# Hybrid decoder trunk on one core: factors spread by split products, mixer sums kept as rows, recurrence tiles five apart

## The chip, the core and the metric

The kernel runs on one NeuronCore of a Trainium2 chip. TensorE (PE in the profile) multiplies, VectorE (DVE), ScalarE (ACT) and GpSimd (POOL) do the elementwise work, SyncE (SP) and ACT issue the DMAs. Each engine runs its own queue in order, and the engines wait for each other through semaphores. The metric is the device time of one execution in microseconds (us); less is better.

## The reference

Two layers, each of three sub-layers with an RMSNorm before and after: a SwiGLU feed-forward, a mixer, a second feed-forward. All arithmetic is float32; x has 1024 features, the hidden layer of a feed-forward 2816.

```python
def layer(x, st_h, st_conv, st_gla, reset_first, p):
    h = rmsnorm(x, p['norm_pre'][0])
    x = x + 0.5 * rmsnorm(swiglu(h, gate0, up0, down0), p['norm_post'][0])
    h = rmsnorm(x, p['norm_pre'][1])
    m, h_last, new_conv, S_fin = mixer(h, st_h, st_conv, st_gla, reset_first, p)
    x = x + rmsnorm(m, p['norm_post'][1])
    h = rmsnorm(x, p['norm_pre'][2])
    x = x + 0.5 * rmsnorm(swiglu(h, gate1, up1, down1), p['norm_post'][2])
```

The mixer projects h to 20 blocks of 128 columns and a low-rank part of 16 columns. Blocks 0 to 3 go through a causal convolution of width 4, two block-diagonal gates and a linear recurrence, and are multiplied with GeLU of blocks 4 to 7 and normalized over 512 features. Blocks 8 to 19 are q, k, v and the output gate of a gated linear attention with 4 heads in chunks; its decay comes from the low-rank part; each head's output is normalized over 128 features. Both parts together go through the output projection. There are 512 prompt tokens and 8 sequences of 8 sample tokens.

## The kernel before

**Tokens and operands.** The 576 tokens are split into two groups g of 288. Everything is held transposed: 128 features on the partitions, 288 tokens along the free axis. A float32 product is made of three fp32r products: each operand is split into a rounded part and the rest (`hh` and `hl` for x, `hidh` and `hidl` for the hidden layer, `wh` and `wl` for weights). ACT makes the rounded part of a weight block (`hi`, L694), DVE the rest (`lo`, L957).

**Units and stages.** A unit is one block of 128 output features: 24 fp32r products of 288 columns (21 where the contraction has 7 tiles). Weight blocks come through a ring of 6; `hi` works 4 units ahead and `lo` 3. Three PSUM banks hold unit results, so unit u waits until the result of unit u-3 is taken, by DVE mostly. `stage_order` lays the units out in stages: for each layer three feed-forward pieces of group 0 (`ffn`), then `ffn` of group 1 with the input projection `win` of group 0 (20 units) among them, `wout` of group 0 (8 units), `win` of group 1, `ffn`, and so on.

**Side work.** What is not a unit product is written as generators that take one step (a slot) after each unit, on each engine's own queue: `recurrence` starts with a `win` stage, `attention` behind it, `boundary` after a sub-layer's last stage. A slot's number fixes the place in each queue; nothing is scheduled at run time. In `recurrence` tile t's convolution, gates and scan lie at slots 4t, 4t+3 and 4t+7. In `attention` the chunk's decay factors are made by ACT at `T_FACTORS`, the keys `kf` by DVE at `T_KEYS` and the slot behind, the queries `qf` by POOL at `T_QUERIES`, and PE transposes values and keys at `T_TRANSPOSES`. `take` on DVE reads a unit's result; `act` is SiLU of the gate on ACT, `hid` the product on DVE.

**Norm factors.** ACT squares, POOL adds the squares up in `ssum`. PE turns them into one column of sums per 96 tokens (`columns`, L428), ACT copies them (`cols`), POOL takes the power -1/2 (`inv`), DVE multiplies it into a diagonal matrix (`diagonal`, L970), and PE multiplies ones by that diagonal in plain fp32 (`spread`, L449), which gives the factor of each token on all partitions. The program holds 44 such spreads: 24 for x and y, and five in each of four mixers.

Of the kernel before, what the change touches and what calls it, by code (L numbers as in the profile page):

```python
# [12 lines left out]
P = 128  # L13
D = 1024
# [47 lines left out]
T_QUERIES = (5, 13, 18)  # L62
T_TRANSPOSES = (7, 15, 23)
T_SCORES = (9, 17, 25)
T_OUTPUTS = (12, 20, 27)
T_SUMS = 30
T_VALUES = T_SUMS + 4

# [90 lines left out]
def program(nc, a, ctx):  # L159
# [36 lines left out]
    diag = [sb(f"diag{s}", [TC, NTC, TC]) for s in range(2)]  # L196
    cols = sb("cols", [TC, 5 * NTC])
    inv = sb("inv", [TC, 5 * NTC])
# [8 lines left out]
    ones = sb("ones", [P, P])  # L207
    means = sb("means", [P, 3])
# [12 lines left out]
    wgdh = sb("wgdh", [P, L, DT * RANK], F32R)  # L221
    wgdl = sb("wgdl", [P, L, DT * RANK], F32R)
    wg2 = sb("wg2", [RANK, L, PR * P])
# [26 lines left out]
    squares, val, eb, qe, gd = [], [], [], [], []  # L250
    for g in range(G):
# [3 lines left out]
        gd.append(sb(f"gd{g}", [RANK, T]))  # L255
# [4 lines left out]
        qe.append(sb(f"qe{g}", [P, PR, C]))  # L260
        assert cursor[0] <= result_at[g] + DT * T * 4
        cursor[0] = result_at[g]
        val.append([sb(f"val{g}{s}", [P, T]) for s in (0, 1)])
# [19 lines left out]
    setup_v, setup_a, setup_p, wgdh_ready, wgdl_ready = (sem(k) for k in ("setup_v", "setup_a", "setup_p", "wgdh_ready", "wgdl_ready"))  # L283
    sq_ready, sq_used = [sem(f"sq_ready{g}") for g in range(G)], [sem(f"sq_used{g}") for g in range(G)]
# [22 lines left out]
    y_stored = sem("y_stored")  # L307

# [11 lines left out]
    def shares_adds(l, st, g):  # L320
        return (l, st) == (L - 1, 2) or (st, g) == (0, 1)

# [12 lines left out]
    def pace(s):  # L335
        if s.kind == "ffn" and s.f == 0 and s.g == 1:
            return 0, 8, 2
        if s.kind == "wout" and s.g == 0:
            return 4, 18, 1
        return 1, 15, 1  # L340

# [19 lines left out]
    def _(e):  # L361
        e.dma_start(raw[0][:, 0:depth(0) * P], a[SOURCES[0][0]][SOURCES[0][1], :, :]).then_inc(raw_landed[0], 16)
        e.dma_start(par[:, :], a["par"]).then_inc(par_landed, 16)
        for u in range(1, RING):
            e.dma_start(raw[u][:, 0:depth(u) * P], a[SOURCES[u][0]][SOURCES[u][1], :, :]).then_inc(raw_landed[u], 16)
        for t, src in ((ident, "ident"), (maskf, "masks"), (seqmask, "seqmask"), (cont, "cont"), (sth, "st_h"), (stc, "st_conv"),
# [28 lines left out]
        for g in range(G):  # L395
            for k in range(4):
# [7 lines left out]
    def _(e):  # L404
        sides = Sides()
        last_use = []
        kept = [0]
        group_event = [0, 0]
# [17 lines left out]
        def columns(src, k, at, first, start, stop):  # L426
            for t in range(NTC):
                mm = e.matmul(psS[0:TC, 0, 288 + at + t:289 + at + t], src[:, t * TC:(t + 1) * TC], means[:, k:k + 1],  # L428
# [7 lines left out]
        def token_sums(g, normed=None):  # L436
            sums_free()
            e.wait_ge(sq_used[g], (DT - 1) * (group_event[g] + 1))
            columns(ssum[g], 0, 0, True, True, True).then_inc(cols_ready, 1)
# [7 lines left out]
        def spread(out, k, count):  # L447
            e.wait_ge(diag_ready, count)
            e.matmul(out, ones[0:TC, :], diag[k][:, :, :], start=True, stop=True).then_inc(spread_done, 1)  # L449

        diags = [0]

        def spread_one():
            spread(psS[:, 0, 0:T], diags[0] % 2, diags[0] + 1)
            diags[0] += 1

        def first_norm(g):
# [6 lines left out]
            spread_one()  # L464

        def boundary(l, st, g, timing, final):
            start, end, at_once = timing
            for slot in range(end + 3):
                if slot == start:
                    token_sums(g, 2 * (3 * l + st) + 2)  # L470
                if slot == start + 2:
# [1194 lines left out]
```

## Time and profile before

| | us |
|---|---|
| median of three runs | 2302.16 |
| lowest and highest | 2298.94, 2306.12 |
| profiled execution, its own time | 2302.01 |
| its span, first to last instruction | 2300.2 |
| PE busy (16988 products) | 2252.3 |
| DVE busy | 1371.8 |
| ACT busy | 1172.6 |
| POOL busy | 722.1 |
| mean granted TensorE clock | 0.981 of full speed |

The span is what the profile can explain; 1.8 us lie around it. A product of 288 columns is busy for about 0.3 us, but a new one starts every 0.13 us, so what a group of products costs is read from the chain of work (its length by its count) and not from the busy time of one. A plain fp32 product appears as two records. An entry in brackets behind a row says how long its engine idled before and for whom.

### The profile page before, as it was taken

Reading aid. Unit: us, or ns where it says so; the run is one execution under the profiler, and the core shown is the slowest. Engines: PE = TensorE matmul, PEld = TensorE weight load, DVE = VectorE, ACT = ScalarE, POOL = GpSimd, SP = SyncE. Lnnn points to the kernel's source line nnn. Section 1 sums busy time; section 2 is a strip of 40 time slices with the busy share of each in tenths; the row PEclk is TensorE's granted clock in tenths of the full one; section 3 lists DMA queues with packets and bytes.
Section 4 is the critical chain, followed back from the end, with each engine's and each line's share of the span. In section 5 each row is a group of like instructions: output and inputs, shape, how many; then the busy total and the mean of one; then the engine's idle time right before and its main releaser. Section 6 shows DMA issues by size and latency. Waiting matters only on the chain.

```text
span 2300.2 us, 40598 instructions
## 1 busy us (share of the span) xinstructions
PE 2252.3 (98%) x16988; PEld 2218.3 (96%) x16988; DVE 1371.8 (60%) x1789; ACT 1172.6 (51%) x1820; POOL 722.1 (31%) x746
## 2 busy tenths in 40 slices
PE   8999999999999999999999999999999999999997
PEld 8999999999899999999999999999998999999997
DVE  6555747647786456655574556675577755576454
ACT  6534547435675345543454355574366653454433
POOL 4112503415354224421251124142254522242112
PEclk9999999989999999999999999999899999999998
DMA  6555555335444455555555555543354443555553
GB/s 214 160 164 163 164 165 156 119 111 166 137 147 128 119 169 157 164 164 164 162 162 163 167 162 159 165 154 122 104 172 138 138 129 114 182 156 165 163 166 118
DMA packets 102244, 350.58 MB, mean 152 GB/s; under 512 B 11296, under 2 KB 16416, under 8 KB 102064
## 3 DMA queue, kind: packets, MB, share of 16 engines
q1 hardware_dynamic: 100976, 346.82, 49.4%
q8 instruction: 135, 2.21, 0.4%
q10 hardware_dynamic: 1088, 1.18, 0.1%
q14 instruction: 45, 0.37, 0.0%
HBM read 343.09 MB, written 4.87 MB: 151 GB/s over the span
## 4 chain that ended last, share of the span: by engine, by line
PE 90%; DVE 7%; ACT 1%; issue 1%; DMA 0%; POOL 0%; DVEq 0%; ACTq 0%; POOLq 0%
PE psD L422 84%; DVE wl L957 2%; DVE kf L1125 1%; PE psS L428 1%; DVE hl L993 1%; PE psM L532 1%; PE psS L449 1%; PE psM L592 1%; PE psM L488 1%; PE psM L508 1%; DMA x<-in_xT 0%; PE psM L581 0%; PE psM L610 0%; DVE y L982 0%; PE psM L449 0%
## 5 line engine op out<-in xcount | busy, mean ns | idle before, releaser
L422 PE MATMUL psD<-hh,wh 128*128 128x288 f32 x3712 | 1124.4, 303 | 14.9 <-DVE hl L993 8.2
L422 PE MATMUL psD<-hl,wh 128*128 128x288 f32 x3712 | 1105.1, 298 | 0.0
L422 PE MATMUL psD<-hh,wl 128*128 128x288 f32 x3712 | 1101.3, 297 | 0.0
L957 DVE TENSOR_TENSOR wl<-raw,wh 128x1024 fp32r<-128x1024 f32 (+1 forms) x656 | 824.2, 1257 | 137.1 <-ACT wh L694 136.8
L694 ACT ACTIVATE wh<-raw 128x1024 fp32r<-128x1024 f32 (+1 forms) x656 | 672.8, 1028 | 145.2 <-DMA raw<-in_w_in 61.8
L422 PEld LDWEIGHTS psD<-hh,wh 128*128 128x128 f32 x3712 | 706.2, 190 | 25.8 <-DVE hl L993 11.1
L422 PEld LDWEIGHTS psD<-hl,wh 128*128 128x128 f32 x3712 | 707.0, 190 | 2.5
L422 PEld LDWEIGHTS psD<-hh,wl 128*128 128x128 f32 x3712 | 708.7, 191 | 0.0
L1565 POOL TENSOR_TENSOR hidl<-hid,hidh 128x288 fp32r<-128x288 f32 x176 | 215.6, 1225 | 974.5 <-ACT hidh L914 974.5
L422 PE MATMUL psD<-hidh,wh 128*128 128x288 f32 x1408 | 421.7, 300 | 0.0
L422 PE MATMUL psD<-hidl,wh 128*128 128x288 f32 x1408 | 416.7, 296 | 0.0
L422 PE MATMUL psD<-hidh,wl 128*128 128x288 f32 x1408 | 416.0, 295 | 0.0
L422 PEld LDWEIGHTS psD<-hidh,wh 128*128 128x128 f32 x1408 | 265.3, 188 | 3.6 <-issue 0.7
L422 PEld LDWEIGHTS psD<-hidl,wh 128*128 128x128 f32 x1408 | 265.7, 189 | 0.5
L422 PEld LDWEIGHTS psD<-hidh,wl 128*128 128x128 f32 x1408 | 266.2, 189 | 0.0
L1354 POOL TENSOR_TENSOR ssum<-ssum,sq 128x288 f32<-128x288 f32 x168 | 188.4, 1123 | 188.5 <-ACT sq L706 185.0
L910 ACT ACTIVATE act<-gate 128x288 f32<-128x288 f32 x176 | 78.4, 445 | 326.7 <-DVE gate L963 326.6
L914 ACT ACTIVATE hidh<-hid 128x288 fp32r<-128x288 f32 x176 | 78.3, 445 | 308.3 <-DVE hid L963 308.3
L963 DVE TENSOR_TENSOR hid<-psD,act 128x288 f32<-128x288 f32 x176 | 80.3, 456 | 255.2 <-PE psD L422 255.2
L963 DVE TENSOR_TENSOR gate<-psD,rstd 128x288 f32<-128x288 f32 x176 | 80.4, 457 | 247.6 <-PE psD L422 247.1
L1302 DVE TENSOR_TENSOR y<-psD,y 128x288 f32<-128x288 f32 x128 | 58.6, 457 | 155.6 <-PE psD L422 155.6
L993 DVE SCALAR_TENSOR_TENSOR hl<-x,par,hh 128x288 fp32r<-128x288 f32 x96 | 88.6, 932 | 2.8 <-ACT hh L724 2.8
(177 smaller groups left out, 1455.2 us busy)
## 6 DMA issues: line engine op xcount, KB each, us to landing
raw<-in_w_gu SPq DMA_DIRECT2D x352, 512.0 KB, 3.6
raw<-in_w_d SPq DMA_DIRECT2D x128, 448.0 KB, 3.2
raw<-in_w_in SPq DMA_DIRECT2D x80, 512.0 KB, 3.6
raw<-in_w_d SPq DMA_DIRECT2D x64, 512.0 KB, 3.6
raw<-in_w_out SPq DMA_DIRECT2D x32, 512.0 KB, 3.6
out_yT<-x SPq DMA_DIRECT2D x8, 288.0 KB, 3.2
gates<-in_w_ax SPq DMA_DIRECT2D x4, 512.0 KB, 4.8
S<-in_st_gla SPq DMA_DIRECT2D x4, 512.0 KB, 4.5
```

What stands on the lines that cost most here:

```text
L422: mm = e.matmul(out, w[:, kt * P:(kt + 1) * P], t[:, kt, :], start=(kt == 0 and part == 0), stop=(kt == KT - 1 and part == 2))
L428: mm = e.matmul(psS[0:TC, 0, 288 + at + t:289 + at + t], src[:, t * TC:(t + 1) * TC], means[:, k:k + 1], start=(first and t == 0), stop=st ...
L449: e.matmul(out, ones[0:TC, :], diag[k][:, :, :], start=True, stop=True).then_inc(spread_done, 1)
L694: e.activation(wh[u % RING][:, 0:width], raw[u % RING][:, 0:width], ACT.Copy).then_inc(hi_ready, 1)
L910: e.activation(act[:, :], gate[:, :], ACT.Silu).then_inc(silu_ready, 1)
L914: e.activation(hidh[:, j, :], hid[:, :], ACT.Copy).then_inc(hidh_ready, 1)
L957: e.tensor_tensor(wl[u % RING][:, 0:width], raw[u % RING][:, 0:width], wh[u % RING][:, 0:width].bitcast(F32), ALU.subtract).then_inc(lo_re ...
L963: e.tensor_tensor(out, bank(u), by, ALU.mult).then_inc(out_taken, 1)
L993: e.scalar_tensor_tensor(hl[g][:, m, :], x[g][:, m, :], col(par, l * NPAR + PRE + st * DT + m), hh[g][:, m, :].bitcast(F32), ALU.mult, ALU ...
L1302: e.tensor_tensor(y[g][:, m, :], bank(u), y[g][:, m, :], ALU.add).then_inc(out_taken, 1)
L1354: e.tensor_tensor(ssum[g][:, :], ssum[g][:, :], sq[g][m % 2][:, :], ALU.add).then_inc(sq_used[g], 1)
L1565: e.tensor_tensor(hidl[:, j, :], hid[:, :], hidh[:, j, :].bitcast(F32), ALU.subtract).then_inc(hidl_ready, 1)
```

## The change

Seven edits are made together.

- **Spreads.** POOL splits `inv` into a rounded part and the rest, DVE makes a diagonal twice as wide (`diag` 96x576), and PE multiplies ones by its halves in two fp32r products. In seven places (`is_quick`, and the first norm of group 0) no diagonal is made: PE multiplies `inv`, read with a broadcast operand, by the identity in three plain fp32 products of 96 columns, one slot after the sums instead of two.
- **Mixer sums.** Instead of 24 one-column products PE makes 8 plain fp32 products of 288 columns whose weights are 5 columns wide, which put five rows of sums into PSUM; ACT copies them, and three transposes one slot later make columns of them.
- **Low rank.** The rounded part and the rest of the 16 weight columns stand side by side, so that 16 products do what 24 did.
- **Recurrence.** Tiles are five units apart instead of four (`R_PERIOD`), with the blocks of `win` in another order. The last tile's work now reaches past the 20 slots of `win`.
- **Attention.** Queries, transposes, scores, outputs and sums come one slot later; values are made two in a slot.
- **Start.** The first two pieces of x are issued by SP behind the first weight block, the parameters and the last two pieces by ACT; 12 warm-up products go.
- **End.** The last square goes straight to PE instead of through POOL's sum, y is rescaled in four pieces, ACT issues the last two stores, and 22 products keep PE going.

```diff
-WARM_UP = [512] * 16 + [256] * 12
+WARM_UP = [512] * 16
+TAIL_WARM = [256] * 12, [256] * 10
-W_IN_ORDER = [0, 4, 8, 9, 1, 5, 10, 11, 2, 6, 7, 16, 3, 17, 18, 19, 12, 13, 14, 15]
+W_IN_ORDER = [0, 8, 9, 10, 11, 1, 4, 5, 6, 7, 2, 16, 17, 18, 19, 3, 12, 13, 14, 15]
+R_PERIOD = 5
+R_END = R_PERIOD * (LT - 1) + 7
-T_QUERIES = (5, 13, 18)
-T_TRANSPOSES = (7, 15, 23)
+T_QUERIES = (6, 14, 18)
+T_TRANSPOSES = (8, 16, 24)
...
+    def is_quick(l, st, g):
+        return (st, g) == (0, 1) or is_final(l, st)
...
         if s.kind == "wout" and s.g == 0:
-            return 4, 18, 1
+            return 3, 18, 1
...
+        def spread(out):
+            k = diags[0] % 2
+            diags[0] += 1
+            e.wait_ge(diag_ready, diags[0])
+            e.matmul(out, ones[0:TC, :], diag[k][:, 0, :, :], start=True, stop=False)
+            e.matmul(out, ones[0:TC, :], diag[k][:, 1, :, :], start=False, stop=True).then_inc(spread_done, 1)
+
+        def spread_quick():
+            e.wait_ge(inv_ready, event[0])
+            for t in range(NTC):
+                mm = e.matmul(psS[:, 0, t * TC:(t + 1) * TC], inv[:, t:t + 1].broadcast_to([TC, P]), ident[0:TC, 0:TC],
+                              start=(t == 0), stop=True, skip_group_check=True)
+            mm.then_inc(spread_done, 1)
...
             for kt in range(DT):
-                for part, (w, t) in enumerate([(wgdh, hh[g]), (wgdh, hl[g]), (wgdl, hh[g])]):
-                    mm = e.matmul(psM[0:RANK, 3, 0:T], w[:, l, kt * RANK:(kt + 1) * RANK], t[:, kt, :],
-                                  start=(kt == 0 and part == 0), stop=(kt == DT - 1 and part == 2))
+                e.matmul(psM[0:2 * RANK, 3, 0:T], wgp[:, l, kt, :], hh[g][:, kt, :], start=(kt == 0), stop=(kt == DT - 1),
+                         skip_group_check=True)
+                mm = e.matmul(psM[0:RANK, 3, 0:T], wgp[:, l, kt, 0:RANK], hl[g][:, kt, :], start=False, stop=(kt == DT - 1),
+                              skip_group_check=True)
...
                     for t in range(LT):
-                        columns(squares[g][:, t, :], 1, 0, t == 0, True, t == LT - 1)
+                        e.matmul(psS[0:STATS, 0, 0:T], pick[:, 0, :], squares[g][:, t, :], start=(t == 0), stop=False)
                     e.wait_ge(head_squared, i + 1)
                     for h in range(HEADS):
-                        mm = columns(vT[:, h, :], 2, (1 + h) * NTC, False, True, True)
+                        mm = e.matmul(psS[0:STATS, 0, 0:T], pick[:, 1 + h, :], vT[:, h, :], start=False, stop=(h == HEADS - 1))
+                    mm.then_inc(rows_ready, 1)
...
-                t = (slot - 5) // 4
-                if slot >= 5 and (slot - 5) % 4 == 0 and t < LT:
+                t = (slot - 5) // R_PERIOD
+                if slot >= 5 and (slot - 5) % R_PERIOD == 0 and t < LT:
...
+            if quick:
+                power.then_inc(inv_ready, 1)
...
+                steps.mark(e.tensor_copy(split[:, 0, 0:width], inv[:, 0:width]))
+                steps.after()
+                e.tensor_tensor(split[:, 1, 0:width], inv[:, 0:width], split[:, 0, 0:width].bitcast(F32), ALU.subtract).then_inc(inv_ready, 1)
```

The change moves instructions at three places that matter below. First ACT's queue behind the `win` stage of group 0 in the first layer. `wh` is a rounded weight block, `rg`, `ig`, `tau`, `aa` and `l` belong to one recurrence tile, `lruo` to GeLU, `gT` to the output gate, `act` and `hidh` to the feed-forward units. Before, these rows lead from the end of `win` into the feed-forward:

```order
L802 ACTIVATE l_146<-l_146 128x288
L805 ACT_TABLE_LOAD
L805 ACTIVATE lruo<-lruo 128x1152
L910 ACT_TABLE_LOAD
L910 ACTIVATE act<-gate 128x288
L694 ACTIVATE wh_61<-raw_67 128x1024
L851 ACTIVATE gT<-gT 128x1152
L914 ACTIVATE hidh<-hid 128x288
L694 ACTIVATE wh_62<-raw_68 128x1024
L910 ACTIVATE act<-gate 128x288
```

In the changed kernel the last recurrence tile stands in the same place, and each change of function brings an `ACT_TABLE_LOAD`:

```order
L981 ACT_TABLE_LOAD
L981 ACTIVATE act<-gate 128x288
L756 ACTIVATE wh_61<-raw_67 128x1024
L844 ACT_TABLE_LOAD
L844 ACTIVATE rg_143<-psM,par 128x288
L845 ACTIVATE ig_144<-psM,par 128x288
L847 ACTIVATE tau_145<-rg_143,sp_99 128x288
L917 ACT_TABLE_LOAD
L917 ACTIVATE gT<-gT 128x1152
L985 ACTIVATE hidh<-hid 128x288
L756 ACTIVATE wh_62<-raw_68 128x1024
L852 ACT_TABLE_LOAD
```

The next rows of the same queue:

```order
L854 ACTIVATE aa_146<-rg_143,nsp_100 128x288
L855 ACTIVATE l_147<-tau_145,tinyc 128x288
L856 ACTIVATE l_148<-tau_145 128x288
L981 ACT_TABLE_LOAD
L981 ACTIVATE act<-gate 128x288
L756 ACTIVATE wh_63<-raw_69 128x1024
L868 ACT_TABLE_LOAD
L868 ACTIVATE l_147<-l_147 128x288
L871 ACT_TABLE_LOAD
L871 ACTIVATE lruo<-lruo 128x1152
L985 ACTIVATE hidh<-hid 128x288
L756 ACTIVATE wh_64<-raw_70 128x1024
```

From the first `act` to the loading of the decay factors (L816 before, L882 now) there were no loads between, and now there are seven; the loading for the factors is the eighth.

Second, DVE's queue in `wout` of group 0 and the start of `win` of group 1, where the boundary of group 1 is handled (`y_56` rescaled, `x_50` added, `hl_54` the operand's rest, `rstd_81` the kept factor, `xlp` the first result taken). Before:

```order
L970 TENSOR_TENSOR diag_89<-ident,inv 96x288
L957 TENSOR_TENSOR wl_76<-raw_70,wh_64 128x1024
L982 TENSOR_TENSOR y_56<-y_56,psS 128x1152
L957 TENSOR_TENSOR wl_71<-raw_65,wh_59 128x1024
L982 TENSOR_TENSOR y_56<-y_56,psS 128x1152
L1027 TENSOR_TENSOR x_50<-x_50,y_56 128x576 x2
L957 TENSOR_TENSOR wl_72<-raw_66,wh_60 128x1024
L957 TENSOR_TENSOR wl_73<-raw_67,wh_61 128x1024
L993 SCALAR_TENSOR_TENSOR hl_54<-x_50,par,hh_53 128x288 x2
L957 TENSOR_TENSOR wl_74<-raw_68,wh_62 128x1024
L993 SCALAR_TENSOR_TENSOR hl_54<-x_50,par,hh_53 128x288 x2
L957 TENSOR_TENSOR wl_75<-raw_69,wh_63 128x1024
```

And now:

```order
L1070 TENSOR_TENSOR y_56<-y_56,psS 128x1152
L1032 TENSOR_TENSOR wl_76<-raw_70,wh_64 128x1024
L1070 TENSOR_TENSOR y_56<-y_56,psS 128x1152
L1074 TENSOR_TENSOR x_50<-x_50,y_56 128x576 x2
L1032 TENSOR_TENSOR wl_71<-raw_65,wh_59 128x1024
L1032 TENSOR_TENSOR wl_72<-raw_66,wh_60 128x1024
L1084 SCALAR_TENSOR_TENSOR hl_54<-x_50,par,hh_53 128x288 x2
L1032 TENSOR_TENSOR wl_73<-raw_67,wh_61 128x1024
L1084 SCALAR_TENSOR_TENSOR hl_54<-x_50,par,hh_53 128x288 x2
L1032 TENSOR_TENSOR wl_74<-raw_68,wh_62 128x1024
L1084 SCALAR_TENSOR_TENSOR hl_54<-x_50,par,hh_53 128x288 x2
```

The diagonal in front is gone, and y, x and the rests `hl` stand one weight block earlier.

Third, PE's queue at the mixer sums of the first layer's group 0. Before:

```order
L422 MATMUL psD<-hl_54,wh_63 128x288
L422 MATMUL psD<-hh_53,wl_75 128x288
L428 MATMUL psS<-means,squares_149 96x1 x12
L428 MATMUL psS<-means,qkv 96x1 x12
L422 MATMUL psD<-hh_53,wh_64 128x288
L422 MATMUL psD<-hl_54,wh_64 128x288
```

And now, with the transposes `rows_153` following one unit later:

```order
L445 MATMUL psD<-hl_54,wh_64 128x288
L445 MATMUL psD<-hh_53,wl_76 128x288
L686 MATMUL psS<-squares_150,pick 5x288 x4
L689 MATMUL psS<-qkv,pick 5x288 x4
L445 MATMUL psD<-hh_53,wh_59 128x288
L445 MATMUL psD<-hl_54,wh_59 128x288
```

Twenty-four products of one column have become eight of 288 columns.

## Rows read from the trace of the kernel before

**Rows 1.** The page's first lines: span, busy time of the engines.

```profile
span 2300.2 us, 40598 instructions
...
PE 2252.3 (98%) x16988; PEld 2218.3 (96%) x16988; DVE 1371.8 (60%) x1789; ACT 1172.6 (51%) x1820; POOL 722.1 (31%) x746
```

**Rows 2.** Chain of work, 1200 to 1500 us: start, length, what.

```profile
...
1210.60 160.14 PE psD L422 x1200
...
1449.55 3.15 PE psM L488 x24
```

**Rows 3.** Chain of work, 795 to 820 us.

```profile
...
801.81 0.48 PE psS L449 x2
```

**Rows 4.** Waits of PE over the span: us in total, times, longest.

```profile
...
PE psM L561 <- DVE kf L1125: 14.4, 8, 2.3
PE psD L422 <- DVE hl L993: 8.2, 12, 1.5
PE psD L422 <- DVE wl L957: 6.7, 3, 2.2
PE psM L508 <- DVE xc L1069: 4.0, 2, 2.0
```

**Rows 5.** Windows from the mixer sums to the spread: length, busy times, PEclk.

```profile
...
505.60:519.30 13.70, 13.70 (x98) 13.70 (x97) 4.64 (x6) 3.06 (x5) 4.78 (x3) 0.75 0.23 69
789.70:801.80 12.10, 12.10 (x98) 12.10 (x97) 4.63 (x6) 3.06 (x5) 4.77 (x3) 0.86 0.32 88
...
sum 51.40, PE 51.40 PEld 51.40 DVE 18.10 ACT 12.45 POOL 18.66; mean PE 12.85 PEld 12.85 DVE 4.53 ACT 3.11 POOL 4.67
```

**Rows 6.** Windows: low rank, second chunk, start of win of group 1.

```profile
...
316.50:319.60 3.10, 3.10 (x26) 2.26 (x24) 2.29 (x5) 1.06 (x1) 0.24 (x2) 1.00 0.59 192
436.00:447.00 11.00, 8.67 (x54) 8.28 (x54) 9.07 (x9) 6.46 (x11) 9.69 (x8) 0.84 0.40 127
594.00:608.00 14.00, 11.76 (x72) 11.10 (x71) 9.05 (x16) 2.12 (x2) 1.57 (x4) 0.88 0.22 75
```

**Rows 7.** Timeline of ACT, 380 to 410 us.

```profile
...
381.91 1.28 ACT L805 ACT_TABLE_LOAD   x1
383.21 1.17 ACT L805 ACTIVATE lruo<-lruo 128x1152 f32<-128x1152 f32 x1
...
386.29 0.45 ACT L910 ACTIVATE act<-gate 128x288 f32<-128x288 f32 x1 [0.61 <-DVE gate L963]
386.64 1.05 ACT L694 ACTIVATE wh<-raw 128x1024 fp32r<-128x1024 f32 x1
...
400.51 1.28 ACT L816 ACT_TABLE_LOAD   x1
...
403.01 1.48 ACT L824 ACTIVATE dec<-dec 128x1536 f32<-128x1536 f32 x1
```

**Rows 8.** Timeline of DVE, 402 to 413 us.

```profile
...
404.52 1.09 DVE L1125 TENSOR_TENSOR kf<-dec,qkv 128x896 f32<-128x896 f32 x1 [1.03 <-ACT dec L824]
...
407.28 2.71 DVE L1125 TENSOR_TENSOR kf<-dec,qkv 128x896 f32<-128x896 f32 x1
```

**Rows 9.** Timeline of PE, 406 to 411 us.

```profile
...
410.05 0.44 PE L561 MATMUL psM<-ident,kf 128*128 128x128 f32 x2 [1.45 <-DVE kf L1125]
```

**Rows 10.** Timeline of DVE, 592 to 601 us.

```profile
...
597.77 0.46 DVE L987 COPY rstd<-psS 128x288 f32<-128x288 f32 x1 [8.45 <-PE psS L449]
```

**Rows 11.** Timeline of PE, 598 to 601 us.

```profile
...
599.97 0.40 PE L422 MATMUL psD<-hh,wh 128*128 128x288 f32 x1 [2.24 <-DVE wl L957]
```

**Rows 12.** Timeline of ACT, 10 to 17 us.

```profile
...
13.72 0.54 ACT L724 ACTIVATE hh<-x,par 128x288 fp32r<-128x288 f32 x1 [1.54 <-DMA x<-in_xT]
```

**Rows 13.** Waits of PE in the first 20 us.

```profile
...
PE psD L422 <- DVE hl L993: 3.4, 4, 1.5
```

**Rows 14.** Timeline of PE, 2280 to 2300.2 us, the end.

```profile
...
2286.79 1.09 PE L428 MATMUL psS<-means,ssum 128*96 128x1 f32 x6 [1.99 <-POOL ssum L1354]
2289.84 1.33 PE L449 MATMUL psS<-diag,ones 96*128 96x288 f32 x2 [1.96 <-DVE diag L970]
```

More of the change, by code:

```diff
@@ L476, in boundary @@
                     token_sums(g)
-                if slot == end + 2:
-                    spread_one()
+                if slot == end + hop:
+                    spread_one(quick)
                 yield
@@ L493, in recurrence @@
             i, g = s.mixer, s.g
-            for slot in range(4 * LT):
+            for slot in range(R_END):
                 if slot == 1:
                     low_rank(s)
-                t = slot // 4
-                if slot % 4 == 3:
+                t = slot // R_PERIOD
+                if slot % R_PERIOD == 3 and t < LT:
                     q = LT * i + t
@@ L615, in attention @@
             i, g = s.mixer, s.g
-            for slot in range(38):
+            for slot in range(T_VALUES + 2):
                 for c, at in enumerate(T_TRANSPOSES):
@@ L847, in attention @@
             i, g = s.mixer, s.g
-            for slot in range(T_VALUES + DT):
+            for slot in range(T_VALUES + DT // 2):
                 if slot == 0:
-                    e.wait_ge(*taken(s.first + 15))
+                    e.wait_ge(*taken(s.first + W_IN_ORDER.index(19)))
                     e.activation(gT[:, :, :], gT[:, :, :], ACT.Silu).then_inc(g_ready, 1)
@@ L1050, in recurrence @@
             gk = vT[:, 2:4, :]
-            for slot in range(4 * LT + 6):
-                t = slot // 4
+            for slot in range(R_END + 3):
+                t = slot // R_PERIOD
                 q = LT * i + t
-                if slot % 4 == 0 and t < LT:
-                    e.wait_ge(*taken(s.first + 4 * t))
+                if slot % R_PERIOD == 0 and t < LT:
+                    e.wait_ge(*taken(s.first + R_PERIOD * t))
                     steps.mark(e.tensor_scalar(cv[0][:, :], xlp[:, 0:W], col(par, pk + CONVW + t), col(par, pk + CONVB + t), ALU.mult, ALU.add))
@@ L1165, in attention @@
             i, g = s.mixer, s.g
-            for slot in range(T_VALUES + DT):
+            for slot in range(T_VALUES + DT // 2):
                 for c, at in enumerate(T_KEYS):
@@ L1385, in first_norm @@
                 yield
-            sizes.append(1)
-            root(NTC, keep=g)
+            root(NTC, keep=g, quick=not g)
             yield
@@ L1425, in recurrence @@
             i, l, g = s.mixer, s.l, s.g
-            for slot in range(4 * LT + 9):
+            for slot in range(R_END + 6):
                 if slot == 0:
@@ L1511, in attention @@
             i, g = s.mixer, s.g
[L1512 removed]
+            for slot in range(T_VALUES + DT // 2 + 1):
                 for c, at in enumerate(T_EXPONENTS):
```

397 lines of the change are left out of this document (242 added, 155 removed).

## Prediction

> **What bounds the kernel now.** I read the page's busy times first, then the chain of work, then PE's waits, then the granted clock by windows. PE is busy for 2252.3 of 2300.2 us, DVE for 60% of the span [rows 1], and the chain is nearly all PE: 1200 unit products take 160.14 us, 0.1335 each [rows 2], so a unit of 24 takes 3.2 us, and the program's 640 units' worth, 15,360 products, take 2050 us. A product is priced by this pace. An edit can gain in three ways only: fewer or cheaper products, less idle time of PE, fewer stretches at the lower clock. PE's idle time is small, and here it is in full for units and keys: 14.4 us for `kf`, 8.2 for `hl`, 6.7 for `wl`, 4.0 for `xc` [rows 4]. After such a wait the clock often falls. The 11 us window around the second chunk's keys has a mean clock of 0.84: 0.16 x 11 x 2 = 3.5 us at the lower level, 1.2 GHz, of which half, 1.7 us, is lost [rows 6]. I call that a dip. The sum is made against the profiled execution, 2302.0 (span 2300.2 and 1.8 around it), which is 0.15 under the median shown.
>
> **Spreads.** Now 0.48 us [rows 3]; two fp32r products of 288 columns cost 2 x 0.1335 = 0.27, so 0.21 less. Of 44 spreads 7 are of the quick kind: three plain fp32 products with 288 columns in all, as many as now, hence about 0.48, no change. 37 x 0.21 = **-8**. DVE's wider diagonal and POOL's two splits are paid in the two units (6.4 us) between sums and spread; without that cover each would cost about 1 us.
>
> **Low rank.** 24 products take 3.15 us [rows 2]; 16 take 2.1. Four times: **-4**. Their weights are 16 and 32 columns wide; the window of today's 16-column ones has clock 1.00 [rows 6], so no fall is expected.
>
> **Mixer sums.** From the first sum to the end of the spread the four windows take 51.4 us, two of them 13.70 at clock 0.75 and 12.10 at 0.86 [rows 5]. At full clock these two would take 13.70 x (1 - 0.25) = 10.3 and 12.10 x 0.86 = 10.4; the other two are alike, so some 10 us of the 51.4 is low clock. The new form is 8 plain products of 288 columns, 8 x 0.48 [rows 3] = 3.9, three transposes of 5 x 96 (288 columns in all, so at most 0.48; I take 0.3), and two units, 6.4: 10.6 each, 42.4 together. If the clock holds, **-9**. Whether it holds no row shows. For it: low-rank products, narrow in weights too, ran at 1.00. Against: what stands here now falls. Bounds: -9, and about 0 if as much is at the lower level as now. I take the first, being nearest to the low-rank row.
>
> **Second-chunk keys.** PE waits up to 2.3 us for `kf`, eight times [rows 4]: four mixers, two chunks. The first chunks take about 1.5 [rows 9], so the second ones have 14.4 - 6 = 8.4. `T_TRANSPOSES` goes a unit (3.2 us) later while the keys stay, so these waits go, with two of the dips: 8.4 + 2 x 1.7 = **-12**. Bounds -14 and -7.
>
> **First-chunk keys.** This is the main cost. `R_PERIOD` pushes tile 3 beyond `win`, where ACT now has slack; the order shows seven table loads between the first `act` and the load for the decay factors, which is the eighth. Today the first `act` starts at 386.29 [rows 7] and `dec` ends at 404.49, with ACT idle between. Now ACT must do: 8 loads x 1.28 = 10.2; 5 `wh` x 1.0 = 5.0; GeLU and `gT`, 1.15 each [rows 7] = 2.3; seven functions of tile 3 at 0.45 (the time of `act`, the same shape) = 3.2; four of `act` and `hidh` = 1.6; factors 0.9 besides `dec` 1.5 = 2.4: 24.7 us, so `dec` ends at 411.0, 6.5 later. Behind it stand `kf` 1.09, gate and `wl` about 1.7, second `kf` 2.71 [rows 8]: 5.5, so keys are ready at 416.5. PE would come to the transposes at 408.6 (410.05 less its 1.45 wait [rows 9]) plus 3.2 = 411.8, and loses 4.7 where it now loses 1.45: +3.3, part of it already in earlier units, which wait for `gate` and `hid` behind ACT. Four times +13, and a dip behind most, +3: **+16**. Bounds: if ACT's late work is covered elsewhere, the slot that is gained takes 4 x 1.5 away, -6; if every load stalls its neighbours, +30.
>
> The second `kf` takes 2.71 us against 1.09 for the first, on the same shape [rows 8], with POOL's `qf` beside it in the trace. The Trainium skill ("GPSIMD Engine Reference") has DVE and POOL share their way to SBUF. By it, moving `qf` a slot later frees the second `kf`, and each first chunk would be 1.6 us better; but the order puts the first `qf` beside the second `kf` again, and the sum keeps 2.71.
>
> **Group 1.** `rstd` is taken at 597.77 [rows 10], and PE then waits 2.24 us for the `wl` behind it [rows 11]: two of three `wl` waits are here, 4.5 us. The `xc` waits are 4.0 us [rows 4]. Of `hl`'s 8.2 us, 3.4 is in the first 20 us [rows 13], leaving 4.8. Together 13.3 us idle, and a dip behind four of these, two `wl` and two `xc` (0.88 in such a window [rows 6]), 6.8. The boundary now ends a unit earlier, the take and its `lo` (2.3 us) fit into a unit, and tiles five apart give `xc` another 3.2 us. That is -20 in full; the quick spread adds a wait for `inv` with no unit between, some 0.6 us twice, and `xc` may keep part: **-17**. Bounds -20 and -6.
>
> **Start and end.** ACT idles 1.54 us for x [rows 12], and PE waits 3.4 us for `hl` [rows 13]. x on another queue may save most: **-3**, bounds -4 and +2 (weight blocks behind x). At the end PE waits 1.99 us for POOL's sum and 1.96 for the diagonal [rows 14]; one goes, warm products only help the clock: **-2**, bounds -4 and 0.
>
> **Sum.** -8 -4 -9 -12 +16 -17 -3 -2 = -39; 2302.0 - 39 = **2263**.
>
> **The rivals.** *The pile-up stays on ACT* (0.18): DVE's `hid` is not late since `act` goes ahead of the loads, and PE's extra unit covers the rest. Then +16 becomes -6 and the time is near 2242. For it: today PE reaches the keys late by only 1.45 us. Against: the 24.7 us counted above are more than the time to the transposes.
>
> *The clock falls under the row products* (0.24): -9 becomes 0, or +8 if they run wholly at 1.2 GHz and double: 2273 to 2281. For it: today's sums fall to 0.75 and 0.86 [rows 5]. Against: low rank at 1.00 [rows 6].
>
> *The pile-up costs more than it saves* (0.04), the slower side: it happens in ACT's queue behind `win` of group 0. Each of seven new loads would have to hold ACT for longer than its record. Slower begins where each mixer loses some 11 us more than I count (39 + 7 by 4). The timeline shows a load of 1.28 us at 381.91 and the next function at 383.21 [rows 7], 0.02 after its end. The Trainium skill ("ScalarE: Activation LUTs", What ACT_TABLE_LOAD costs) adds a drain of about 1380 ns to each switch; by that rule this would be 8 x 1.38 = 11 us more per mixer and 44 in all, an estimate of 2307. The trace disagrees: load to next function is 1.30 us here, not 2.66, hence the small chance.
>
> *Clock falls and the waits of group 1 stay* (0.04): 2281 + 12 = 2293, nearly no change.
>
> The forecast itself, all terms about as sized, has 0.50 and reaches from 2252 to 2277.
>
> **How the numbers follow.** The range runs from the middle of the first rival (2240) to above the second (2284): about 1 in 10 lies below, in the first rival's lower half, and 1 in 10 above, in the last two and a worse second. A measurement tells 0.3%, some 7 us, from no change. Only the last two rivals reach 2295: faster 0.92, same 0.04, slower 0.04.
>
> **What the next profile would show.** Right: spread pairs 0.27 us apart to the next unit; low rank 2.1; the sums' clock near 1.00; no waits at second chunks; waits of 4 to 5 us at first chunks, with seven loads on ACT ahead of them; no `wl` wait where `win` of group 1 starts. Wrong: a clock near 0.75 over the row products; no PE wait for the first chunk; `hid` or `gate` waits in many units behind `win`; an `hl` wait at group 1 as large as before since `inv` is late. The prediction fails most easily by the size of the first-chunk term, whose bounds are 36 us apart.

## The result

The changed kernel takes 2288.7 us (median of four runs, 2287.8 to 2292.8) against 2303.2 before; the ratio is 0.9939, interval 0.9927 to 0.9952. It is faster by 14 us, not by the 39 that I forecast, and lies outside the range of 2240 to 2284. The profiled execution has a span of 2286.0 us, 14.2 less than before. The page of the changed kernel, in the same lines as [rows 1]:

```profile
span 2286.0 us, 40462 instructions
...
PE 2238.6 (98%) x16890; PEld 2199.2 (96%) x16890; DVE 1371.3 (60%) x1787; ACT 1193.0 (52%) x1840; POOL 727.3 (32%) x793
```

PE's busy time falls by 13.7 us, its share of the span stays. Now PE's waits over the span, to be read beside [rows 4]:

```profile
...
PE psD L445 <- DVE wl L1032: 12.6, 9, 2.3
PE psM L616 <- DVE kf L1220: 8.5, 4, 2.5
PE psS L483 <- DVE diag L1046: 6.4, 4, 1.7
PE psM L563 <- DVE xc L1164: 4.5, 2, 2.3
PE psD L445 <- DVE hl L1084: 2.4, 4, 1.5
PE psD L445 <- DMA ident<-in_ident: 2.0, 1, 2.0
```

Four things changed. `hl` fell from 8.2 to 2.4 us. `kf` fell from 14.4 to 8.5, four waits and not eight: the second chunks have none. `wl` rose from 6.7 us in three places to 12.6 in nine. And `diag`, awaited once before, at the end [rows 14], now has 6.4 us in four places within the mixers, which my sum put at nothing.

Where the time went shows when the same unit starts in both timelines of PE. I cut PE's 15,360 unit products into 640 groups of 24, call the n-th group unit n, and take four kinds of stretch, with all their places added up:

| stretch | before | changed | difference | forecast |
|---|---|---|---|---|
| behind `win`, keys of both chunks (units 110 to 134, 182 to 204, 430 to 454, 503 to 525) | 364.5 | 370.5 | +6.0 | +16 - 12 = +4 |
| mixer sums and five spreads (134 to 146, 204 to 217, 454 to 466, 525 to 537) | 224.5 | 229.7 | +5.2 | -9 - 4 = -13 |
| boundary of group 1 and its `win` (156 to 177, 476 to 497) | 178.3 | 157.9 | -20.5 | -17, low rank -2, spreads -1 |
| first three units, from the start | 28.4 | 28.1 | -0.4 | -3 |

The last row ends where unit 3 starts, at 28.43 and 28.07. The third row flatters the change: 1.5 us of its 20.5 are gate products of the last recurrence tile, which now come just behind unit 177. The miss of 25 us is for the most part in one row, the mixer sums: 18 us.

### The profile page after: what moved, and what is told of

Same layout as the page of the kernel before. It is cut to its first block, busy times and chain, and to the rows that moved or that the text cites. A ratio compares the mean times of both kernels' runs of the same rounds, so it can differ in the third digit from the quotient of the medians.

```text
span 2286.0 us, 40462 instructions
## 1 busy us (share of the span) xinstructions
PE 2238.6 (98%) x16890; PEld 2199.2 (96%) x16890; DVE 1371.3 (60%) x1787; ACT 1193.0 (52%) x1840; POOL 727.3 (32%) x793
## 4 chain that ended last, share of the span: by engine, by line
PE 87%; DVE 6%; ACT 5%; POOL 1%; issue 1%; DMA 0%; SPq 0%; DVEq 0%; POOLq 0%
PE psD L445 81%; DVE wl L1032 2%; ACT wh L756 1%; DVE hl L1084 1%; PE psM L587 1%; PE psM L563 1%; DVE kf L1220 1%; POOL inv L1467 1%; DVE diag L1046 1%; DVE y L1070 1%; PE psM L647 1%; PE psM L665 1%; PE psM L636 0%; PE psS L451 0%; ACT L981 0%
## 5 line engine op out<-in xcount | busy, mean ns | idle before, releaser
L445 PE MATMUL psD<-hh,wh 128*128 128x288 f32 x3712 | 1117.3, 301 | 17.2 <-DVE wl L1032 12.6
L1682 POOL TENSOR_TENSOR hidl<-hid,hidh 128x288 fp32r<-128x288 f32 x176 | 211.0, 1199 | 966.4 <-ACT hidh L985 966.4
L1454 POOL TENSOR_TENSOR ssum<-ssum,sq 128x288 f32<-128x288 f32 x166 | 193.4, 1168 | 173.4 <-ACT sq L768 169.5
```

The lines of the kernel that those rows point to most:

```text
L445: mm = e.matmul(out, w[:, kt * P:(kt + 1) * P], t[:, kt, :], start=(kt == 0 and part == 0), stop=(kt == KT - 1 and part == 2))
L1454: e.tensor_tensor(ssum[g][:, :], ssum[g][:, :], sq[g][m % 2][:, :], ALU.add).then_inc(sq_used[g], 1)
L1682: e.tensor_tensor(hidl[:, j, :], hid[:, :], hidh[:, j, :].bitcast(F32), ALU.subtract).then_inc(hidl_ready, 1)
```

## Inside the row that failed

The windows of the changed kernel, as in [rows 5] and [rows 6] (length, busy times, PEclk): the low rank products, the attention's last products with the unit behind, the row sums with a unit, and the unit behind the spread.

```profile
...
315.50:317.70 2.20, 2.20 (x19) 1.72 (x19) 2.14 (x4) 0.76 (x1) 0.00 (x0) 1.00 0.39 119
494.00:501.00 7.00, 7.00 (x44) 6.67 (x41) 0.00 (x0) 0.00 (x0) 0.00 (x0) 0.51 0.00 0
508.00:515.50 7.50, 7.50 (x43) 4.62 (x42) 1.59 (x2) 1.95 (x4) 2.59 (x2) 1.00 0.20 61
525.00:529.00 4.00, 4.00 (x21) 4.00 (x20) 2.19 (x3) 1.17 (x2) 0.00 (x0) 0.59 0.02 4
```

The low rank takes 2.1 us from unit to unit at clock 1.00, as forecast. The row sums, 508.0 to 512.1, also run at 1.00, and no stretch at 1.2 GHz follows, where one of 6.8 us followed the columns before. So the clock held, and the forecast of -9 seemed in good order. What spoils it comes three units later. The chain of work, 505 to 535 us:

```profile
...
510.17 1.94 PE psS L689 x8
512.11 3.41 PE psD L445 x24
...
516.38 0.94 ACT wh L756
517.32 0.07 ACT cols L778
...
517.46 2.75 POOL inv L1467
...
520.26 0.52 POOL split L1475
...
520.85 0.23 POOL split L1477
...
521.10 3.40 DVE diag L1046 x2
...
524.63 0.41 PE psM L483
```

Read it from the rows (ended at 512.1) on. A unit passes, then the transposes; ACT has `wh` ahead of `cols`; POOL's power on 15 columns takes 2.75 us, its two split steps 0.5 and 0.2, and DVE's two diagonals 3.40, of which the first, the one that PE's first spread needs, takes 2.71. PE had come to the spread at 522.3 and waits:

```profile
...
523.87 0.40 PE L483 MATMUL psS<-diag,ones 96*128 96x288 f32 x1 [1.55 <-DVE diag L1046]
```

There are three units between sums and spread, where there were two, but the transposes take the first. The two that are left, 6.6 us, do not hold a chain of 8.4 (515.4 to 523.8). My forecast said that the split steps "are paid in the two units (6.4 us) between sums and spread; without that cover each would cost about 1 us". I never summed the chain. A stretch at 1.2 GHz follows, from 525 here, in three of the four mixers.

One link of the chain is longer than it is elsewhere in this trace. These rows are DVE's two pairs of diagonals and what POOL does beside the first pair:

```profile
...
521.10 3.38 DVE L1046 TENSOR_TENSOR diag<-ident,split 96x576 fp32r<-96x576 f32 x2 [0.39 <-POOL split L1477]
...
525.77 1.41 DVE L1046 TENSOR_TENSOR diag<-ident,split 96x576 fp32r<-96x576 f32 x2
```

```profile
...
521.03 0.81 POOL L1682 TENSOR_TENSOR hidl<-hid,hidh 128x288 fp32r<-128x288 f32 x1
521.80 1.41 POOL L1649 TENSOR_TENSOR gT<-gT,oT 128x576 f32<-128x576 f32 x1
```

The same wide diagonal takes 0.75 us where POOL does nothing beside it, 1.37 beside `hidl` alone and 2.71 beside `hidl` and `gT`, in all four mixers alike. At 0.75 it would have ended at 521.85 (an estimate), before PE came at 522.3. So the wait may need two things, a chain without room and POOL's next work beside the diagonal. No run takes the second away, so its share is not shown; the next run gives the chain more room.

## Experiments on the mixer sums

**Spreads one unit later.** The edit, on the changed kernel:

```diff
-T_VALUES = T_SUMS + 4
+T_VALUES = T_SUMS + 5
-                if slot == T_SUMS + 3:
+                if slot == T_SUMS + 4:
                     spread_one()
-                    if slot == T_SUMS + 3 + (h + 1) // 2:
+                    if slot == T_SUMS + 4 + (h + 1) // 2:
                         spread(psM[:, h, 0:T])
```

DVE's last three diagonals move by a slot as well.

> The changed kernel with its five mixer spreads, and the values behind them, one unit later (PE, DVE, ACT and POOL alike); the sums and their transposes stay. Theory: the rows take a unit of their own for the transposes, so of three units between sums and spread only two are left for cols, inv, two split steps on POOL and two diagonals of 96x576 on DVE, some 8 us; PE waits 6.4 us for diag in four places and each wait brings a stretch at 1.2 GHz worth 1.7 us. It expects no wait for diag and four stretches less: 6.4 + 6.8 = 13 us less than 2288.7, so 2275 to 2277. Rival: POOL and DVE are held up by other work of the feed-forward there and the wait moves along with the spread: 2288.

Measured: 2278.9 us, 9.8 less than the changed kernel; ratio to before 0.9891 (0.9876 to 0.9905). The first waits of PE, in order of size:

```profile
...
PE psD L445 <- DVE wl L1032: 12.6, 9, 2.3
PE psM L616 <- DVE kf L1220: 8.5, 4, 2.5
PE psM L563 <- DVE xc L1164: 4.5, 2, 2.2
```

No wait for `diag` is left, and the others are as they were. The four stretches of the mixer sums take 216.2 us instead of 229.7. The theory holds. The span fell by 11.0 and not by 13.5; 1.5 us of the rest are a stretch at 1.2 GHz that this execution has at the boundary of group 1 in the second layer. The first diagonal takes 2.73 us here too. Against the kernel before these stretches are now 8.4 us shorter, where the sum has 13. Of the missing 4.6, 1.6 are in the products: with what they hold up of the unit behind, rows take 4.2 us and transposes 0.4, forecast as 3.9 and 0.3. Another 1.7 are stretches at 1.2 GHz behind the attention's last products, which last 27.4 us in all here and 23.9 before. The rest I did not follow.

**Columns again.** The changed kernel with one-column sums, `cols` and the power directly behind them:

```diff
-                        e.matmul(psS[0:STATS, 0, 0:T], pick[:, 0, :], squares[g][:, t, :], start=(t == 0), stop=False)
+                        for j in range(NTC):
+                            at = 288 + j * STATS
+                            e.matmul(psS[0:TC, 0, at:at + 1], squares[g][:, t, j * TC:(j + 1) * TC], pick[:, 0, 0:1], ...)
```

> The changed kernel with the mixer sums made by 24 one-column products again, ACT's cols and POOL's root directly behind them, spreads where they are. Theory (as for the later spreads): the waits for diag go, 6.4 us and four stretches of 1.7, since cols start a unit earlier; against that each mixer pays 0.9 us more for the products and gets back the stretch at 1.2 GHz that stood behind the one-column products in the kernel before (3.4 us where it is 6.8 long, 1.7 where it is 3.4): 2286 to 2292. Rival one, the rows gave the full 2.2 us per mixer that I forecast and the wait for diag comes from the split alone: the wait stays and the time rises to 2297. Rival two, the clock does not depend on the form of the sums: 2279.

Measured: 2293.5 us (0.9956, 0.9941 to 0.9971), 4.8 more than the changed kernel, between the theory and rival one. The wait did not go as a whole:

```profile
...
PE psM L483 <- DVE diag L1041: 5.8, 4, 1.4
```

The first spread is in time, but the second one, whose diagonal stands behind the first in the same slot of DVE, is 1.4 us late. The width alone does not do it: in the run with split spreads on the kernel before (below), where each spread has a slot of its own, no mixer waits for `diag`. Here the first two share a slot, which belongs to the change's edit of the attention. So this run mixes effects, and I made the clean one below.

**Columns where nothing waits.** Both kernels with tiles four apart and late spreads (see the next section), this one with columns:

> The kernel of tiles four apart and late mixer spreads, with one-column mixer sums. There is no wait for diag in either, so it prices the rows alone. Theory: 24 products of one column take 0.9 us more per mixer than 8 of 288 columns, and the chip grants 1.2 GHz behind them for 3.4 to 6.8 us in most mixers, 1.7 to 3.4 us lost: 2248 plus 9 to 14, about 2259. Rival: the clock falls as often behind rows as behind columns and only the 3.6 us remain: 2252.

Measured: 2256.7 us against 2248.0 with rows: rows are worth 8.7 us, just under the 9 to 14 that I expected. The same window in both, first columns, then rows:

```profile
...
502.00:509.00 7.00, 7.00 (x38) 7.00 (x39) 0.00 (x0) 0.27 (x1) 3.48 (x4) 0.54 0.01 6
```

```profile
...
502.00:509.00 7.00, 7.00 (x48) 5.75 (x46) 1.59 (x2) 1.84 (x4) 1.41 (x2) 1.00 0.16 52
```

The columns' 7 us run at 0.54, those of the rows at 1.00. It is the clock alone that pays: at full clock, in the second mixer of the kernel before, the 24 columns cost 4.1 us, less than rows and transposes (4.6), and not 0.9 more as I expected. The stretches behind the columns last 20.4 us in the kernel before, of which half, 10.2, is lost. The forecast term of -9 was right in size and in its cause; it was overlaid by the wait.

**Split spreads alone, on the kernel before.** POOL's two steps, the wide diagonal and two fp32r products everywhere:

```diff
-            e.matmul(out, ones[0:TC, :], diag[k][:, :, :], start=True, stop=True).then_inc(spread_done, 1)
+            e.matmul(out, ones[0:TC, :], diag[k][:, 0, :, :], start=True, stop=False)
+            e.matmul(out, ones[0:TC, :], diag[k][:, 1, :, :], start=False, stop=True).then_inc(spread_done, 1)
```

> The kernel before with nothing but the split spreads (POOL's two steps, the wide diagonal, two fp32r products), in all 44 places but none quick. Theory: each spread is 0.21 us cheaper, 9 us in all, where boundaries have two units between sums and spread; in the four mixers, whose first two diagonals stand in one slot, DVE ends the second some 1.5 us late (as with the one-column sums in the changed kernel, 5.8 us in all): 2294 plus 0 to 6, about 2298. Rival: the cover holds everywhere, 2294. Second rival: two fp32r products are no cheaper than one plain product, 2303 or more.

Measured: 2304.4 us (1.0000, 0.9988 to 1.0012), no change, where I expected 2298. In the timeline a spread on the path does gain its 0.21 us: between units 217 and 391, where no mixer is, 1.8 us less in the changed kernel. What ate the gain in this kernel is partly visible:

```profile
...
PE psS L450 <- DVE diag L972: 3.7, 3, 2.8
```

Three waits for `diag`, 3.7 us, none of them in a mixer, where there was one of 1.96 at the end [rows 14]; that one is 2.8 now. So the 1.5 us a mixer that I expected did not come. The rest is the clock: its granted mean is 0.977 against 0.981 before, and 0.4% of 2300 is 9 us. Ten runs of this one kernel lie between 2294.1 us at clock 0.982 and 2308.4 at 0.975. Why the chip grants less here is not settled.

## Experiments on the recurrence

**Tiles four apart.** The changed kernel with two lines of before:

```diff
-W_IN_ORDER = [0, 8, 9, 10, 11, 1, 4, 5, 6, 7, 2, 16, 17, 18, 19, 3, 12, 13, 14, 15]
-R_PERIOD = 5
+W_IN_ORDER = [0, 4, 8, 9, 1, 5, 10, 11, 2, 6, 7, 16, 3, 17, 18, 19, 12, 13, 14, 15]
+R_PERIOD = 4
```

> The changed kernel with recurrence tiles four units apart and the old order of win; everything else changed stays. Theory: the pile-up on ACT behind win of group 0 and 1 costs 10.8 us of waits for wl, 8.5 for kf and three stretches of 1.7, and all of it comes from tile 3 standing beyond win; the gain at group 1 comes from the boundary that ends earlier. It expects 24 us less, about 2265. Rival: tiles five apart also give group 1 its gain (DVE's backlog in win of group 1 is the recurrence's), so waits for wl and xc come back there with stretches, some 10 to 14 us: 2275 to 2279. Second rival: the wait for first-chunk keys has another source (POOL's qf beside the second kf, 2.7 us), then kf keeps its 8.5: 2276 or more.

Measured: 2260.2 us (0.9807, 0.9791 to 0.9824), 28.6 less than the changed kernel. PE's first waits:

```profile
...
PE psS L483 <- DVE diag L1046: 6.4, 4, 1.7
PE psM L563 <- DVE xc L1164: 4.0, 2, 2.0
PE psD L445 <- DVE hl L1084: 3.3, 5, 2.0
PE psD L445 <- DVE wl L1032: 2.3, 1, 2.3
```

The first row of the table falls from 370.5 to 344.1 us, which is nearly the whole gain. `kf` is gone altogether and `wl` keeps the one wait of the start. `xc` still has 4.0 us, in the changed kernel 4.5: five apart gave `xc` nothing, and both rivals are wrong.

**The same edit on the kernel before,** tiles five apart and nothing else:

> The kernel before with nothing but tiles five apart and the new order of win; transposes, spreads and sums as before. Theory: the pile-up behind win costs each mixer 2.7 us of wl waits, and the first-chunk keys are 3.2 us shorter of room than in the changed kernel, so PE waits 5.3 us for them where it waits 1.5; a stretch of 1.7 behind most: 8 us per mixer, 32 in all, 2335; second chunks keep their waits. Rival: the extra unit in win relieves DVE and gives back 10 us at group 1 (xc and wl waits): 2325. Second rival: the pile-up matters only together with the later transposes: 2310.

Measured: 2341.0 us, 38 more than before; ratio 1.0161 (1.0147 to 1.0175). This part alone makes the kernel slower.

```profile
...
PE psM L563 <- DVE kf L1127: 26.8, 8, 5.7
PE psD L424 <- DVE wl L959: 18.2, 13, 2.2
PE psD L424 <- DVE hl L995: 8.6, 13, 1.5
...
PE psM L510 <- DVE xc L1071: 1.7, 4, 0.6
```

`kf` is waited for up to 5.7 us, `wl` for 18.2 in all. `xc` does fall here, from 4.0 [rows 4] to 1.7, and group 1, with the gate products that move behind unit 177 counted in, is 3 us shorter. It pays for neither: the sum is 38 us where I expected 32. The mean clock is 0.972.

**What is late behind `win`.** Timeline of ACT in the changed kernel, 392 to 410 us, its loads and the factors:

```profile
...
392.14 1.28 ACT L852 ACT_TABLE_LOAD   x1
...
394.75 1.28 ACT L981 ACT_TABLE_LOAD   x1
...
397.46 1.28 ACT L868 ACT_TABLE_LOAD   x1
...
399.21 1.28 ACT L871 ACT_TABLE_LOAD   x1
...
402.97 1.28 ACT L981 ACT_TABLE_LOAD   x1
...
405.68 1.28 ACT L882 ACT_TABLE_LOAD   x1
...
408.18 1.47 ACT L890 ACTIVATE dec<-dec 128x1536 f32<-128x1536 f32 x1
```

The order forecast seven loads ahead of the factors' one; six of the eight stand here, and the other two just before. From the start of a load to its next function it is 1.29 or 1.30 us at each of them, as in [rows 7]. The Trainium skill ("ScalarE: Activation LUTs", What ACT_TABLE_LOAD costs) has 2.66 us for a switch; this trace does not agree. From the first `act` at 384.34 to the end of `dec` at 409.65 it is 25.3 us, forecast 24.7. PE waits:

```profile
...
402.44 0.40 PE L445 MATMUL psD<-hh,wh 128*128 128x288 f32 x1 [2.12 <-DVE wl L1032]
...
415.20 0.44 PE L616 MATMUL psM<-ident,kf 128*128 128x128 f32 x2 [2.46 <-DVE kf L1220]
```

Three runs ask what holds it up. The first takes GeLU out:

```diff
-                if slot == R_END:
+                if slot == 19:
```

> The changed kernel with only GeLU moved: ACT makes it at slot 19 of win, before tile 3, and not behind it. One table load and 1.16 us of GeLU leave the pile-up behind win. Theory: the factors are ready 2.4 us earlier, the second kf ends about when PE comes to the transposes, so the wait for kf (8.5 us in all) and its stretches at 1.2 GHz (three of 1.7) go: 2275 to 2278. Rival: what is late is DVE's kf beside POOL's qf, which starts with them: the wait for kf stays above 5 us in all and the time is 2285 to 2289.

Measured: 2287.1 us (0.9927, 0.9912 to 0.9942), some 2 us less; `kf` still 5.8. The theory fell. ACT now idles instead:

```profile
...
398.70 0.45 ACT L868 ACTIVATE l<-l 128x288 f32<-128x288 f32 x1
401.23 0.44 ACT L985 ACTIVATE hidh<-hid 128x288 fp32r<-128x288 f32 x1 [2.09 <-DVE hid L1038]
```

ACT's `hidh` waits 2.09 us for DVE's `hid`, which stands behind the scan, which waits for ACT's root at 398.70. So I formed another theory, that this exchange is the cause, and moved the root and DVE's scan:

```diff
-                t = (slot - 7) // R_PERIOD
+                t = (slot - 8) // R_PERIOD
```

> The changed kernel with one thing moved: ACT's root (the exponential of half the logarithm) and DVE's product and scan behind it stand one slot later for every recurrence tile. Theory, formed since GeLU's move brought only 2 us: behind win ACT and DVE wait for each other in turn; DVE's hid and the lo behind it stand behind the scan, which waits for ACT's root and its table load, and ACT's next work waits for that hid. One slot later hid goes first; then the waits for wl behind win (10.8 us in six places) fall below 4 us, while the factors come no earlier and kf keeps about its 8.5: about 2281. Rival, ACT is simply out of time there (24.7 us of work, as I had forecast): waits for wl shrink but kf's grow by as much, and the time stays at 2288.

Measured: 2283.7 us (0.9908, 0.9890 to 0.9926), 5 less by the medians and nothing by the span (2286.3). Its four runs lie between 2276.9 and 2288.1, and the profiled one is the slowest of them. `wl` has 14.8 us and `kf` 7.7: the waits stay, a unit later. This theory fell too as it stood. ACT has no idle time in this trace from 388 to 404.9. Then both edits together:

> The changed kernel with GeLU at slot 19 of win and the root one slot later, both edits of the single runs together. Theory: two chains of about equal length stand behind win, ACT's own queue (contiguous from 388 to 405 us in the run with the late root) and the exchange in which DVE's hid waits for ACT's root (2.0 us of idle ACT in the run with the early GeLU); with both shortened the waits for wl and kf behind win, 19 us in all now, fall to about 10, and the time to 2275 to 2278. Rival: something else sets it, the waits stay above 16 us, and the time is 2282 to 2287.

Measured: 2278.4 us (0.9894, 0.9878 to 0.9911), 10 less than the changed kernel.

```profile
...
PE psM L616 <- DVE kf L1220: 10.8, 4, 2.7
...
PE psD L445 <- DVE wl L1032: 4.6, 7, 2.3
```

The stretches of the table's first row say it best, as they leave out what the clock does elsewhere: GeLU 1.1 less, the root 1.2 more, both 8.5 less (370.5 to 362.0). By the medians it is 1.7, 5.0 and 10.4 less. This fits two chains of about equal length behind `win`, ACT's own queue and the exchange of ACT and DVE, of which each hides the gain of the other; the lengths themselves I did not trace. The late root also takes `xc` from 4.5 to 2.8 us. The waits behind `win` fall from 18.8 us (8.5 for `kf` and 12.6 less the start's 2.3 for `wl`) to 13.1, short of the 10 that I expected.

## Putting it together

**Tiles four apart and late spreads:**

> Tiles four apart with the old order of win, and the mixer's spreads one unit later: the two edits of the runs before together. Theory: the waits for diag (6.4 us, four stretches) and those behind win are independent, so 2260 less 11 is 2249. Rival: with tiles four apart DVE and POOL meet other work there and part of the wait stays: 2254 to 2260.

Measured: 2248.0 us (0.9759, 0.9743 to 0.9774), 40.7 less than the changed kernel, of which the two edits alone bring 28.6 and 9.8. They add up to 38.4, so within the noise they are independent.

**The attention's slots back by one** in this kernel (`T_TRANSPOSES = (7, 15, 23)` and its companions):

> The same kernel with queries, transposes, scores, outputs and sums back in their slots of before, one unit earlier. Theory: the extra unit ahead of the transposes is what removed the waits for kf at both chunks, since with tiles four apart the factors come as early as before; it expects the 14.4 us of kf waits of the kernel before again with two stretches of 1.7, so 18 us more, 2267. Rival: only the second chunks gain by it, 8.4 and 3.4, 2261. Second rival: the spread edits had changed DVE's order enough, 2250.

Measured: 2267.0 us, 19 more.

```profile
...
PE psM L616 <- DVE kf L1220: 14.4, 8, 2.3
```

That is the 14.4 us of [rows 4] to the tenth. It fits my term for the second chunks (-12), and the same step would have taken the first chunks' 6 us too, had the tiles stayed where they were.

**The boundary of group 1 by a diagonal again,** in this kernel:

```diff
-        return (st, g) == (0, 1) or is_final(l, st)
+        return is_final(l, st)
```

> The same kernel (tiles four apart, late mixer spreads) with the boundary of group 1 behind the first feed-forward made by a diagonal again, two units behind its sums, and so one unit later; the final norms and the first one stay quick. Theory: the gain of some 10 us per layer at group 1 is this one unit: hl waits of 4.8 us, wl waits of 4.5 and two stretches of 1.7 come back, less 1.5 for the quick form's waits for inv: 11 us more, 2260. Rival: the earlier order of squares (POOL adds one slot later, low rank shorter) brought it: 2250.

Measured: 2250.9 us, 2.8 more, and 5.8 more by the span, where I expected 11. The waits do come back:

```profile
...
PE psD L445 <- DVE wl L1032: 6.7, 3, 2.3
PE psD L445 <- DVE hl L1084: 4.7, 10, 1.3
```

`wl` again has 6.7 us; `hl` has 4.7, not the 8.2 of before. But no stretch at 1.2 GHz follows them here (the window from 579 to 583 has clock 1.00). In the kernel before one followed the same `wl` wait [rows 6]. A wait does not always cost its stretch.

**Two more edits:** the gates' products one unit later, and PE's wait for the identity matrix only ahead of the first spread:

```diff
-                t = slot // R_PERIOD
-                if slot % R_PERIOD == 3 and t < LT:
+                t = (slot - 4) // R_PERIOD
+                if slot >= 4 and (slot - 4) % R_PERIOD == 0 and t < LT:
                     q = LT * i + t
                     e.wait_ge(xc_ready, q + 1)
```

> Tiles four apart, late mixer spreads, and two more edits: PE makes the gates' products one unit later (xc waits, 3.8 us and two stretches), and PE waits for the identity matrix only ahead of the first spread (1.6 us at the start). Theory: both waits go and nothing takes their place, 2248 less 5 to 9, about 2241. Rival: ACT reads the gates a slot behind PE, now in the same slot, and is late with the root; DVE and the keys follow: 2248 or more.

Measured: 2245.7 us (0.9742, 0.9729 to 0.9756), 2.3 less, below the 5 to 9 that I expected; the runs of the two kernels overlap (2242.2 to 2246.6 and 2244.9 to 2249.7).

```profile
...
PE psD L445 <- DVE wl L1033: 4.5, 3, 2.3
PE psD L445 <- DVE hl L1085: 4.4, 8, 1.7
```

`xc` is gone from the waits, and `wl` has 2.2 us more than the start's own: what waited for DVE's `xc` now waits for DVE's `wl`, as DVE is the late one. The wait for the identity matrix is gone too, but `hl` has 4.4 us where it had 3.3, and unit 3 starts at 27.96, no earlier than in the changed kernel. It is the fastest kernel of the study, 2.6% faster than before and 1.9% than the change.

## Why the prediction was wrong

- **The sum failed at the spreads' cover,** in the step "paid in the two units (6.4 us) between sums and spread". In the mixers the transposes take a unit of their own, and cols, power, split and the first diagonal need 8.4 us where two units give 6.6. Shown by the spreads moved by a unit: 9.8 us by the medians, 13.5 in the four stretches. Part of it was to be had from the trace of before, where POOL's power takes 2.74 us and DVE's pair of diagonals 2.65 (the first 1.06), and from the order's third place, which puts the transposes a unit behind the sums. That the first wide diagonal would take 2.71 us beside POOL no row of before showed.
- **Spreads and low rank:** 0.27 and 2.1 us a piece, as forecast. The quick form costs 0.8 us more than the diagonal did at each boundary of group 1 (33.7 us from unit 146 to 156, 32.9 before), where I forecast 0.6.
- **Mixer sums:** -9 forecast, 8.7 measured with nothing waiting. Right in the clock, which holds over and behind the row products. That narrow weights are the reason, as with the low rank, was an analogy and no run tests it. The rival "the clock falls under the row products", to which I gave 0.24, did not occur.
- **Second-chunk keys:** right. **First-chunk keys:** +16 together with -12 against +6.0 measured in these stretches, so +18, right in place and nearly in size. The wait for the keys itself is only 2.5 us, and up to 2.1 us at once for `wl` stand ahead of it, where I forecast 4.7 in one. But I took the loads' sum for the only chain, which the GeLU run refutes. And what I did not see is what it meant to keep tiles five apart: against tiles four apart it costs 28.6 us, as it also throws away the first chunks' 6 us.
- **Group 1:** -20.5 in the table; with the gate products behind (+1.5) and the quick spreads ahead (+1.6) it is -17.3, where the sum has -20 with its share of low rank and spreads. So the size was nearly right. The share I gave to tiles five apart was wrong: `xc` went from 4.0 to 4.5 in the changed kernel. Only on the kernel before, with its boundary, does five apart help `xc` (1.7).
- **Start:** -0.4 instead of -3. PE waits 2.0 us for the identity matrix, a wait that the change itself puts there, and 1.8 for `hl`. **End:** 3.0 less (14.2 less the 11.2 that the last unit starts earlier), forecast 2.
- The terms above explain the 25 us: 18 in the mixer sums, 3 in group 1 with its quick spreads, 3 at the start, 2 behind `win`, less 1 at the end. Start and end were read from the timelines alone; no run takes them out by themselves.

## What to carry over

When a step is put into a chain that ends in another engine's fixed slot (a transposition, a split, a wider operand), sum the whole chain from the first result to the waiting instruction and hold it against the units between, engine by engine; a cover that was never full is no cover for more. When a large change moves the time little, undo its parts one by one from both ends: here six parts together were worth -43 (2303.2 to 2260.2) and the seventh +29. And where a removed load brings nothing, look for idle time that took its place before dropping the theory; two chains of equal length need two edits.

## What the runs showed of the hardware

TensorE's clock fell to 1.2 GHz behind the attention's last small products in all four mixers of every kernel here (0.51 in the window from 494 to 501 above); no term of my sum counts these stretches. It also fell behind many waits of about 2 us, though not behind all: the wait of 2.46 us at 415.2 was followed by such a stretch, the one of 2.12 us at 402.4 was not. The 24 products of one column at the mixer sums brought one in each of the 20 mixers of the five kernels with columns; the six of the other norms brought none between units 217 and 391. Plain fp32 products of 288 columns with 5-column weights brought none in the 40 mixers of the ten kernels with rows. Between runs of one kernel such stretches come and go: 2294.1 us at a mean clock of 0.982 and 2308.4 at 0.975. A part of 9 us, such as the split spreads alone, is smaller than this spread of 14 and can't be read from single times; in the timeline, from unit to unit, its 0.21 us a piece can.

DVE's wide diagonal, the same instruction on 96x576 elements, took 0.75 us with POOL idle, 1.37 with POOL's `hidl` beside it and 2.71 with `hidl` and `gT` beside it, in the changed kernel. That POOL is the reason fits all these places, but no run moves it away.
